# The opening stage of a one-layer hybrid decoder kernel: wide row pieces for the modulation sum, x scaled on ScalarE, and two dense blocks by k tile among the transposes

## The reference, cut to what matters

```python
mod = (silu(c) @ w_ada + b_ada)          # c: 1 x 1024, w_ada: 1024 x 6144
sh1, sc1, g1, sh2, sc2, g2 = split(mod, 6)
h = rms_norm(x) * (1 + sc1) + sh1        # x: 1024 x 1024
proj = h @ w_in                          # 1024 x 10528, block by block
```

## Time and profile before

| | |
|---|---|
| median of 3 runs | 3126.21 us (3120.81 to 3139.49) |
| the profiled execution | 3130.62 us, of which the span of its instructions is 3128.7 us |
| TensorE busy | 94% of the span |
| VectorE busy | 47% |
| ScalarE, GpSimd busy | 23% each |
| mean granted TensorE clock | 0.965 of full speed |

### The profile page before, as it was taken

The page is one execution under the profiler, slowest core; times in us unless marked ns, Lnnn a source line. Parts: engine busy times, 40 slices in busy tenths (PEclk is TensorE's granted clock), DMA queues, the critical chain, the costliest instruction groups (busy, mean ns, idle before and its releaser), DMA issues.

```text
span 3128.7 us, 61733 instructions
## 1 busy us (share of the span) xinstructions
PE 2925.8 (94%) x25747; PEld 2390.7 (76%) x25747; DVE 1459.3 (47%) x1815; ACT 706.5 (23%) x1004; POOL 726.0 (23%) x454
## 2 busy tenths in 40 slices
PE   1899999999999999999989997988999999999998
PEld 1688879787878788866657775877777888888886
DVE  6555464544554545485853556445524222222222
ACT  1222121212121212144444665010112000000001
POOL 0212120203020211122312100333232333333331
PEclk7999999999999999999999998999998999999999
DMA  5111111101020101143331102243421111111111
GB/s 180 49 44 36 38 42 31 46 27 60 13 70 23 50 30 35 45 116 91 110 88 45 48 14 71 89 137 128 141 64 44 53 48 47 47 47 49 51 47 68
DMA packets 247066, 192.75 MB, mean 62 GB/s; under 512 B 21729, under 2 KB 225083, under 8 KB 246843
## 3 DMA queue, kind: packets, MB, share of 16 engines
q1 hardware_dynamic: 239136, 163.02, 17.6%
q10 hardware_dynamic: 7707, 26.34, 2.1%
HBM read 158.91 MB, written 30.41 MB: 61 GB/s over the span
## 4 chain that ended last, share of the span: by engine, by line
PE 84%; DVE 8%; ACT 4%; issue 3%; DMA 1%; ACTq 0%; DVEq 0%; POOL 0%; SPq 0%; POOLq 0%
PE ps L246 59%; PE ps L776 2%; PE ps L790 2%; PE ps L787 2%; PE ps L754 2%; DVE arena L1446 1%; PE ps L839 1%; PE ps L870 1%; PE ps L871 1%; DVE arena L1671 1%; PE ps L956 1%; PE ps L981 1%; PE ps L969 1%; PE ps L724 1%; PE ps L723 1%
## 5 line engine op out<-in xcount | busy, mean ns | idle before, releaser
L246 PE MATMUL ps<-x_hi,w_hi 128*128 128x512 f32 (+1 forms) x2576 | 838.8, 401 | 39.0 <-issue 13.9
L246 PE MATMUL ps<-x_lo,w_hi 128*128 128x512 f32 (+1 forms) x2576 | 821.5, 394 | 0.0
L246 PE MATMUL ps<-x_hi,w_lo 128*128 128x512 f32 (+1 forms) x2576 | 819.6, 394 | 0.0
L236 POOL CAST w_hi<-w_raw 128x1024 fp32r<-128x1024 f32 (+2 forms) x221 | 222.6, 1007 | 2343.7 <-PE ps L246 1608.5
L246 PEld LDWEIGHTS ps<-x_hi,w_hi 128*128 128x128 f32 (+1 forms) x2576 | 486.3, 191 | 177.5 <-issue 62.6
L246 PEld LDWEIGHTS ps<-x_lo,w_hi 128*128 128x128 f32 (+1 forms) x2576 | 490.8, 191 | 104.3
L246 PEld LDWEIGHTS ps<-x_hi,w_lo 128*128 128x128 f32 (+1 forms) x2576 | 489.1, 190 | 106.5
L238 POOL TENSOR_TENSOR w_lo<-w_raw,w_hi 128x1024 fp32r<-128x1024 f32 (+2 forms) x221 | 487.9, 2208 | 17.7
L1896 DVE TENSOR_TENSOR arena<-ps,arena 128x1024 f32<-128x1024 f32 x22 | 26.9, 1225 | 392.8 <-PE ps L246 392.8
L1913 DVE SCALAR_TENSOR_TENSOR arena<-ps,mod,arena 128x1024 f32<-128x1024 f32 x88 | 113.0, 1284 | 129.9 <-PE ps L246 129.9
L1613 DVE COPY_PREDICATED arena<-hid_lo,ps 128x256 f32<-128x256 int32 x144 | 72.2, 501 | 139.1 <-PE ps L787 88.5
(11 more groups left out here) (268 smaller groups left out, 3611.6 us busy)
## 6 DMA issues: line engine op xcount, KB each, us to landing
w_raw<-in_w_in SPq DMA_DIRECT2D x78, 512.0 KB, 3.9
w_raw<-in_w_ffn_in SPq DMA_DIRECT2D x44, 512.0 KB, 3.8
arena<-in_w_ada SPq DMA_DIRECT2D x32, 512.0 KB, 3.7
gates_sig<-arena ACTq DMA_DIRECT2D x24, 512.0 KB, 2.7
arena<-gates_sig SPq DMA_DIRECT2D x24, 512.0 KB, 3.4
w_raw<-in_w_ffn_out SPq DMA_DIRECT2D x22, 512.0 KB, 3.5
arena<-in_x SPq DMA_DIRECT2D x16, 512.0 KB, 6.3
arena<-in_w_ada SPq DMA_DIRECT2D x8, 1024.0 KB, 12.0
```

The costliest lines, as they stand in the source:

```text
L236: nc.gpsimd.tensor_copy(hi, raw).then_inc(s_whi, 1)
L246: ins = nc.tensor.matmul(dst[h], wp, xp[h], start=first and m == 0, stop=last and m == 2)
```

## The change

- w_ada's first 2048 columns are loaded as 16 pieces of 128 rows x 1024 columns (one k tile's rows, half of the columns; 512 KB in runs of 4 KB), into 12 slots. Five semaphores cover pieces 0-4, 5-8, 9-12, 13-14 and 15. Two accumulators of 1024 columns are used in turn, so VectorE makes 2 `tensor_scalar` and 14 `scalar_tensor_tensor` of 128x1024. TensorE adds the partitions in three steps: columns 0-7 of `mod` (after piece 14), then 8-9, then 10-15 (after piece 15).
- The 1 for sc1 is added to b_ada's part at once, ahead of the sums.
- The raw weights of lora 0 and 1 are loaded ahead of x.
- `s_x` becomes two semaphores, of four tiles each. ScalarE takes the squares before the exponential, makes the root with the division and the epsilon in it, and scales x itself (eight `Copy` with a scale per partition, after VectorE's reciprocal, which stands behind VectorE's first five pieces). TensorE's first transposes wait for the eighth.
- Lora 0 and 1 run together by k tile: transposes of k tile k+2, then six matmuls of lora 0 and six of lora 1 for k tile k. Lora 2 follows as before.

```diff
             engine_sems[engine] += got
             return got if len(got) > 1 else got[0]
-        s_x = sem("x_loaded")
+        s_x = [sem(f"x_loaded_{k}") for k in range(2)]
         p0_pe, p0_act, p0_dve = made_by("pe", "start_pe"), made_by("act", "start_act"), made_by("dve", "start_dve")
         ada_out, ada_pe = made_by("dve", "mod_columns_ready"), made_by("pe", "mod_columns_done")
-        ADA0, ADA_SLOTS, ADA1 = 8, 7, 32
-        s_ada = [sem(f"ada_weights_loaded_{k}") for k in range(ADA_SLOTS)]
+        ADA0, ADA_SLOTS = 2 * KT, 12
+        ADA_PARTS = [(0, 5), (5, 9), (9, 13), (13, 15), (15, 16)]
+        s_ada = [sem(f"ada_weights_loaded_{k}") for k in range(len(ADA_PARTS))]
+        ADA_COLS = [(0, 8), (8, 10), (10, 16)]
         ada_acc = made_by("dve", "ada_products_summed")
         acc_steps = made_by("dve", "ada_product_steps")
         s_mod = sem("modulation_inputs_loaded")
...
             return w[:, bass.ds(c0, n)].rearrange("(k p) m -> p k m", p=P)
-        st0 = carve([("row_rw", P), ("row_lru", P), ("row_mod", P), ("xs", 8 * D), ("tmp", 2 * T), ("acc", 2 * 256),
-                     ("ada", ADA_SLOTS * 2048)])
-        ada_w0 = st0["ada"].rearrange("p (s k m) -> p s k m", s=ADA_SLOTS, k=KT)
+        st0 = carve([("row_rw", P), ("row_lru", P), ("row_mod", P), ("xs", 8 * D), ("tmp", 2 * T), ("acc", 2 * 1024),
+                     ("ada", ADA_SLOTS * 1024)])
+        ada_w0 = st0["ada"].rearrange("p (s m) -> p s m", s=ADA_SLOTS)
         ada_acc0 = st0["acc"].rearrange("p (s m) -> p s m", s=2)
         row_rw, row_lru, row_mod = st0["row_rw"], st0["row_lru"], st0["row_mod"]
         xs = st0["xs"].rearrange("p (t d) -> p t d", t=8)
...
         def _(sp):
             sp.dma_start(keep[:, :], a["consts"][:, 0:C_KEEP]).then_inc(s_const, 16)
             w_in, w_ada = a["w_in"][0], a["w_ada"][0]
+            for c, (c0, w) in enumerate(((0, P), (P, P))):
+                load_block(sp, Block("lora", c), cols(w_in, COL_LORA + c0, w), w)
             for t in range(8):
-                sp.dma_start(xs[:, t, :], a["x"][0, t * P:(t + 1) * P, :]).then_inc(s_x, 16)
-            for n in range(ADA0):
-                if n >= ADA_SLOTS:
-                    sp.wait_ge(ada_acc, upto(n - ADA_SLOTS + 1))
-                sp.dma_start(ada_w0[:, n % ADA_SLOTS, :, :], cols(w_ada, n * 256, 256)).then_inc(s_ada[n % ADA_SLOTS], 16)
-                if n == ADA_SLOTS - 1:
-                    for c, (c0, w) in enumerate(((0, P), (P, P))):
-                        load_block(sp, Block("lora", c), cols(w_in, COL_LORA + c0, w), w)
+                sp.dma_start(xs[:, t, :], a["x"][0, t * P:(t + 1) * P, :]).then_inc(s_x[t // 4], 16)
+            for part, (n0, n1) in enumerate(ADA_PARTS):
+                for n in range(n0, n1):
+                    if n >= ADA_SLOTS:
+                        sp.wait_ge(ada_acc, upto(n - ADA_SLOTS + 1))
+                    src = w_ada[n // 2 * P:(n // 2 + 1) * P, n % 2 * 1024:(n % 2 + 1) * 1024]
+                    sp.dma_start(ada_w0[:, n % ADA_SLOTS, :], src).then_inc(s_ada[part], 16)
             load_block(sp, Block("lora", 2), cols(w_in, COL_LORA + 2 * P, 32), 32)
             load_gains(sp)
...
                     ins = pe.transpose(ps[:, 4 + 2 * (k % 2) + t // 4, (t % 4) * P:(t % 4 + 1) * P], xs[:, t, k * P:(k + 1) * P], ident)
                 ins.then_inc(h_pe, 1)
-            pe.wait_ge(p0_dve, upto(16))
+            pe.wait_ge(p0_act, upto(18))
             for k in range(2):
                 transpose_x(k)
-            for n in range(ADA0):
-                pe.wait_ge(ada_acc, upto(n + 1))
-                pe.wait_ge(ada_out, upto(n - 1))
-                for c in range(2):
-                    ins = mm(ps[:, 2 + n % 2, c:c + 1], ada_acc0[:, n % 2, c * P:(c + 1) * P], ones[:, 0:1], start=True, stop=True)
+            for part, (c0, c1) in enumerate(ADA_COLS):
+                half = c0 // 8
+                pe.wait_ge(ada_acc, upto(ADA0 - 1 + half))
+                for c in range(c0, c1):
+                    ins = mm(ps[:, part, c:c + 1], ada_acc0[:, half, c % 8 * P:(c % 8 + 1) * P], ones[:, 0:1], start=True, stop=True)
                 ins.then_inc(ada_pe, 1)
-            for k in range(2, KT):
-                pe.wait_ge(h_tmp, upto(k - 1))
-                transpose_x(k)
-            dense(pe, Block("lora", 0), ready=(h_lo, 0, 1))
-            dense(pe, Block("lora", 1))
+            lora = [Block("lora", c) for c in range(2)]
+            for blk in lora:
+                pe.wait_ge(s_wsplit, upto(blk.before + 1))
+            pe.wait_ge(ada_out, upto(3))
+            for k in range(KT):
+                if k + 2 < KT:
+                    pe.wait_ge(h_tmp, upto(k + 1))
+                    transpose_x(k + 2)
+                pe.wait_ge(h_lo, upto(k + 1))
+                for blk in lora:
+                    w = [t[:, blk.slot, k * P:(k + 1) * P] for t in (w_hi, w_lo)]
+                    x = [[t[:, k, h * 512:(h + 1) * 512] for h in range(2)] for t in (x_hi, x_lo)]
+                    ins = three_passes([ps[:, 2 * blk.slot + h, :] for h in range(2)], w, x, k == 0, k == KT - 1)
+                    if k == KT - 1:
+                        ins.then_inc(s_dense, 1)
             pe.wait_ge(a_xp, upto(1))
             dense(pe, Block("lora", 2), width=32)
             pe.wait_ge(a_wa, upto(3))
...
             load_parameters(act)
             act.wait_ge(p0_dve, upto(4))
             fn(mod[:, 48:56], mod[:, 48:56], ACT.Silu).then_inc(p0_act, 1)
+            for t in range(8):
+                if t % 4 == 0:
+                    act.wait_ge(s_x[t // 4], 16 * 4)
+                if t >= 2:
+                    act.wait_ge(p0_act, upto(t))
+                fn(sq0[:, t % 2, :], xs[:, t, :], ACT.Square, accum_out=sumsq[:, t:t + 1]).then_inc(p0_act, 1)
+            act.wait_ge(p0_act, upto(9))
+            act.wait_ge(p0_dve, upto(5))
+            fn(rstd, sumsq, ACT.Sqrt, scale=1.0 / D, bias=eps_rms).then_inc(p0_act, 1)
+            act.wait_ge(p0_dve, upto(9))
+            for t in range(8):
+                fn(xs[:, t, :], xs[:, t, :], ACT.Copy, scale=rstd[:, t:t + 1]).then_inc(p0_act, 1)
             act.wait_ge(lam_s, upto(2))
             fn(rate2, rate, ACT.Exp, scale=-1.0).then_inc(p0_act, 1)
-            for t in range(8):
-                act.wait_ge(s_x, 16 * 8)
-                if t >= 2:
-                    act.wait_ge(p0_act, upto(t + 1))
-                fn(sq0[:, t % 2, :], xs[:, t, :], ACT.Square, accum_out=sumsq[:, t:t + 1]).then_inc(p0_act, 1)
-            act.wait_ge(p0_dve, upto(7))
-            fn(rstd, rstd, ACT.Sqrt).then_inc(p0_act, 1)
             for k in range(KT):
                 act.wait_ge(h_tmp, upto(k + 1))
                 fn(x_hi[:, k, :], h_tmpb[:, k % 2, :], ACT.Copy).then_inc(h_hi, 1)
...
                 step(v.memset(row, 0.0))
             dve.wait_ge(p0_pe, upto(1))
             step(v.tensor_copy(mod[:, :], ps[:, 6, 0:56]))
+            step(v.memset(eps_rms, 1e-6))
+            step(v.tensor_scalar(mod[:, MOD_SC1:MOD_SC1 + 8], mod[:, MOD_SC1:MOD_SC1 + 8], 1.0, None, ALU.add))
             for k, dst in enumerate((rw_par, lru_par)):
                 dve.wait_ge(p0_pe, upto(k + 2))
                 step(v.tensor_copy(dst[:, :], ps[:, 4 + k, 0:P]))
...
                         ins = v.scalar_tensor_tensor(acc, w[:, k, :], c_k, acc, ALU.mult, ALU.add)
                     ins.then_inc(acc_steps if k < KT - 1 else ada_acc, 1)
-            def ada_add(n):
-                dve.wait_ge(ada_pe, upto(n + 1))
-                cols2 = mod[:, 2 * n:2 * n + 2]
-                v.tensor_tensor(cols2, ps[:, 2 + n % 2, 0:2], cols2, ALU.add).then_inc(ada_out, 1)
-            dve.wait_ge(p0_act, upto(10))
-            step(v.tensor_scalar(rstd, sumsq, 1.0 / D, 1e-6, ALU.mult, ALU.add))
-            dve.wait_ge(p0_act, upto(11))
-            step(v.reciprocal(rstd, rstd))
-            for t in range(8):
-                step(v.tensor_scalar(xs[:, t, :], xs[:, t, :], rstd[:, t:t + 1], None, ALU.mult))
             dve.wait_ge(p0_act, upto(1))
-            for n in range(ADA0):
-                dve.wait_ge(s_ada[n % ADA_SLOTS], 16 * (n // ADA_SLOTS + 1))
-                if n >= 2:
-                    dve.wait_ge(ada_pe, upto(n - 1))
-                ada_sum(ada_acc0[:, n % 2, :], ada_w0[:, n % ADA_SLOTS, :, :], (KT - 1) * n)
-                if n >= 1:
-                    ada_add(n - 1)
-            ada_add(ADA0 - 1)
-            dve.wait_ge(ada_out, upto(ADA0))
-            v.tensor_scalar(mod[:, MOD_SC1:MOD_SC1 + 8], mod[:, MOD_SC1:MOD_SC1 + 8], 1.0, None, ALU.add).then_inc(ada_fix, 1)
-            dve.wait_ge(ada_fix, upto(1))
+            for part, (n0, n1) in enumerate(ADA_PARTS):
+                for n in range(n0, n1):
+                    c_k, acc = mod[:, 48 + n // 2:49 + n // 2], ada_acc0[:, n % 2, :]
+                    if n == n0:
+                        dve.wait_ge(s_ada[part], 16 * (n1 - n0))
+                    if n < 2:
```

(25 more changed lines are left out.)

12 lines of the change are left out of this document (6 added, 6 removed).

## The result

The changed kernel's median is 3093.23 us (3083.56 to 3106.5, 4 runs), against 3131.31 for the kernel before (4 runs). The ratio is 0.9872, with a 95% interval of 0.9843 to 0.9901: 1.3% less, 40 us. The forecast was 0.75% less, 23.5 us, reckoned from a median of 3126.21; a gain of over 1% had been given a chance of 0.11. The profiled execution of the changed kernel took 3106.5 us (span 3104.7, mean clock 0.970), only 24 less than that of before, and is the slowest of its four runs. So the first question is which of the two differences is the change's.

The account below looks back on a forecast made before the run. VectorE was taken to bound the opening, TensorE the rest. First `modulate` 27.7 us earlier, lora 0 and 1's end 30.7, lora 2's start 25.9, less 2.4 for low clock: 23.5 gained, 3103 us, range 3092 to 3117.

Parts of the forecast that it names:

- M: Start of the first `modulate` in the opening: forecast at 46.0 us, 27.7 earlier than 73.70.
- Rival 1: Opening: the loads or ScalarE come late; gain 17 to 21 us, time 3106 to 3109; chance 0.18.
- rival 4: Modulation sum: wide steps cost as much per element as narrow ones; gain 11 us, time 3115; chance 0.04.
- The loop: Interleaved lora 0 and 1, from 50.1 us: matmuls 22.3, transposes 5.5, low clock at the start 2.0.
- E: End of lora 0 and 1: forecast at 79.9 us, 30.7 earlier than 110.64.
- The tail: VectorE's rate chain, masks and clearing (8.4 us), then ScalarE's copy (1.03), hold lora 2 back 4.8; low clock costs 2.4.
- Rival 2: Ahead of lora 2: VectorE's tail is shorter and no clock falls; E near 78, time 3096 to 3098; chance 0.13.
- First RWKV block: Its start, after lora 2 and a stall: forecast near 105.5 us, 23.5 earlier than 129.06.
- rival 5: Behind the opening: its gain is lost to another phase of loads against matmuls, few microseconds; chance 0.03.
- Rival 3: Interleaved loop and lora 2: TensorE's clock stays low; 9 us slower, time 3135; chance 0.02.

Follow-up runs that it names:

- 7.00 kind: Profiles in which the modulation sum's 16 partition products took 7.00 us, where others took 4.10 to 4.84.
- e2: Changed kernel with all transposes first, then lora 0 and lora 1 one after the other; mean 3097.6 us, ratio 0.9894 to the kernel before.
- e3: Changed kernel with VectorE's tail (rate's chain, clearing, mask copies) and SP's mask load moved into the interleaved loop; mean 3081.7 us, ratio 0.9843.
- e9: Changed kernel with each RWKV turn's four products for g moved from behind the 64 one-column products to behind the next dense block; mean 3081.3 us, ratio 0.9838.
- e4: e3 with TensorE's wait for the last tanh/sigmoid of the lora results moved behind the first RWKV block; mean 3089.6 us, ratio 0.9868.
- e11: Kernel before with the order of e9 in its RWKV turns; mean 3112.7 us, ratio 0.9947.
- e6: Changed kernel with two unused TensorE products added ahead of the RWKV turns; mean 3110.3 us, ratio 0.9934 (with four, the next run: 3107.4, 0.9921).
- e8: Kernel before with four unused TensorE products added ahead of the RWKV turns; mean 3148.9 us, ratio 1.0059.

## Why the prediction was right in the opening and wrong in the total

- **M.** Forecast 46.0, measured 45.61. Loads (24.5 forecast, 25.34 measured), pieces, ScalarE's scaling (9.1 forecast, 8.43 us measured) and the transposes all fell where the sums put them. VectorE began 0.8 late and made it up, since its wide steps follow each other after 1.23 us, not 1.28. That it came within 0.4 us is partly luck: in the profiles of the 7.00 kind M is near 47.6, and the sum has no term for it. Rival 1 and rival 4 fell.
- **The loop.** E was put at 79.9 and was 78.0. The first k tile took 3.81, 1.1 over the later ones, where 2.0 was set down; the transposes cost 0.87 a group, not 1.09. That makes the sum 1.1 + 0.9 too large.
- **The tail.** Forecast gap 4.8, measured 5.02, ended by the copy that VectorE's clearing released. e2 and e3 show it from both sides: without the interleaved loop there is no gap, and with the tail moved it is 0.16. The sum didn't say outright that the interleaving would thereby be worth next to nothing; the comparison of e2 with e9 does. The low clock behind it was set at 2.4 and cost 1.8 (12.79 for the 48 matmuls, 11.0 at full clock, by e4's 96 in 22.12). Rival 2 was right about E (78.0) and wrong about the clock.
- **First RWKV block.** Forecast 105.5, measured 102.73 and 103.11; gain forecast 23.5, measured 26.3.
- **The step that failed** is in the third paragraph of "What bounds the kernel now": "Behind that one nothing is edited, so a gain there is the gain at the end unless something gives it back", and with it rival 5, which had "a matter of few microseconds" and a chance of 0.03. The means differ by 37.7 ± 3.2, the openings by 26.3 (26.0 between e9 and e11), so some 11 us came from a part that nobody edited. e6 to e8 show that this part changes by 10 to 16 us when a little work ahead of it moves its start, and the turn lengths show it as low-clock spells. e9 and e11, which take apart the place where the spells of the turns begin, bring 11.4 to the changed kernel and 17.7 to the one before. So 6 ± 3 of the 11 us are spells that the changed kernel has fewer of; that it has fewer, and not more, is luck as far as the prediction goes, since e4 and e6 to e8 went the other way. The other 5 stay open. The profiles of e9 and e11 don't place them: e11's seven turns took 4.1 us longer and the rest 2.8 shorter. The clock later on (attention, merge) could hold them, but no run separates it.
- **The number 3103.** It was reckoned from 3126.21, the median of three runs; the mean of 83 is 3130.4, from where the same sum gives 3107. The measured 3092.7 is 14 below that: 3 from the opening, 11 from behind it. The median of 3093.23 lies next to the range's low end; taken as the measured ratio on the prediction's own 3126.21, it is 3086, outside.
- **The low end of the range**, 3092, was built on rival 2 and a spread of 4 us between runs. The runs of one kernel spread over 26 us (3080.78 to 3106.5), and this was visible before: 3120.81 to 3139.49 in three runs.
- **Rival 3** fell: the clock was up from the second k tile (2.77 us for its 12 matmuls, 3.81 for the first).

## What to carry to other kernels

When a part is moved in time, ask not only whether its work is untouched, but whether its speed depends on when it starts; the spread between runs of the unedited kernel says how much that can be, and belongs in the range. Compare the lengths of a loop's identical turns, with the granted clock of each, and look at what TensorE did just before the clock fell. Here it was 64 one-column products with four more products behind them, and to put a dense block between the two gave 11 to 18 us and took most of the spread away; whether it does in another loop has to be measured. And when an engine's idle time is filled, look at what it used to have time for afterwards: a chain that was hidden comes to stand at the end of the new, shorter path.
